# GpSimd makes five of the low parts of w_out's second half between and behind its last low parts of w_in

## The reference, cut to what matters

```python
proj = x @ w_in                                  # 1024 -> q | k | v | g | bg | cg | hc, 512 each
q, k = rotary(q), rotary(k) * HEAD_DIM ** -0.5
o, s_ret_new = retention(q, k, v, s_ret)         # chunks for the new stream, one block for the running ones
ret_out = groupnorm(o) * silu(g) * beta_ret
u = cg * hc
z = conv_b + sum(conv_w[t] * upad[:, t:t + L] for t in range(3))
conv_out = bg * z * beta_conv
m = concat([ret_out, conv_out]) @ w_out          # 1024 x 1024
h = layer_norm1(alpha * x + m)
y = layer_norm2(alpha * h + moe(h))              # moe: top 4 of 32, two matrices of 1024x2048 and 1024x1024 each
```

## Time and profile before

| | us |
|---|---|
| median of 3 runs | 1122.45 (1121.52 to 1122.66) |
| the profiled execution: its time | 1123.92 |
| the profiled execution: its span | 1122.1 |

### The profile page before, as it was taken

The page is one execution under the profiler, slowest core; times in us unless marked ns, Lnnn a source line. Parts: engine busy times, 40 slices in busy tenths (PEclk is TensorE's granted clock), DMA queues, the critical chain, the costliest instruction groups (busy, mean ns, idle before and its releaser), DMA issues.

```text
span 1122.1 us, 13598 instructions
## 1 busy us (share of the span) xinstructions
PE 1077.4 (96%) x5552; PEld 543.1 (48%) x5552; DVE 332.1 (30%) x596; ACT 199.1 (18%) x344; POOL 103.0 (9%) x58
## 2 busy tenths in 40 slices
PE   9999999999999999999999999999998989898994
PEld 6889968344434343434443434343434343433431
DVE  3487984512131212121213021212131313121114
ACT  3244213120112020202010102020111111111101
POOL 4675550000000000000000000000000000000002
PEclk9999999999999999999999999999999999999998
DMA  9970298999999999999999999999999999999993
GB/s 351 323 236 1 87 383 339 427 425 427 426 428 428 427 426 429 427 427 428 430 427 429 429 427 428 429 429 428 429 429 426 428 430 429 428 429 428 425 428 143
DMA packets 55748, 436.28 MB, mean 389 GB/s; under 512 B 8032, under 2 KB 18016, under 8 KB 28992
## 3 DMA queue, kind: packets, MB, share of 16 engines
q1 hardware_dynamic: 49184, 428.68, 91.8%
q10 hardware_dynamic: 6528, 7.09, 1.8%
HBM read 431.78 MB, written 3.97 MB: 388 GB/s over the span
## 4 chain that ended last, share of the span: by engine, by line
PE 63%; DMA 27%; DVE 1%; ACT 0%; POOL 0%; issue 0%; DVEq 0%; SPq 0%; ACTq 0%; POOLq 0%
DMA ring<-w_down 24%; PE bank L989 24%; PE bank L1015 17%; PE bank L925 8%; PE bank L622 4%; DMA old_rooms<-w_down 3%; PE bank L1038 1%; PE bank L833 1%; PE bank L1040 1%; PE bank L970 1%; PE bank L998 1%; PE bank L758 1%; PE bank L823 1%; DVE mixed_lo L1521 0%; PE bank L796 0%; PE bank L772 0%
## 5 line engine op out<-in xcount | busy, mean ns | idle before, releaser
L989 PE MATMUL bank<-ring,xg 128*64 128x512 f32 x1536 | 345.5, 595 | 8.9 <-DMA ring<-w_gu 8.9
L989 PEld LDWEIGHTS bank<-ring,xg 128*64 128x64 f32 x1536 | 105.2, 136 | 211.8 <-issue 186.5
L1015 PE MATMUL bank<-ring,act_t 128*64 128x512 f32 x672 | 150.8, 595 | 8.0 <-DMA ring<-w_down 8.0
L989 PE MATMUL bank<-old_rooms,xg 128*64 128x512 f32 x496 | 112.4, 595 | 5.0 <-DMA old_rooms<-w_gu 5.0
L1720 DVE SCALAR_TENSOR_TENSOR oo_lo<-oo_raw,gate_s,oo_hi 128x512 fp32r<-128x512 f32 x32 | 24.0, 751 | 312.7 <-ACT oo_hi L1247 312.7
L1748 DVE TENSOR_SCALAR gate_c<-bank 128x512 f32<-128x512 f32 x32 | 22.1, 692 | 258.6 <-PE bank L989 258.6
L925 PEld LDWEIGHTS bank<-onehot,hid 128*128 128x128 f32 x720 | 85.9, 196 | 12.2 <-issue 12.2
L1015 PEld LDWEIGHTS bank<-ring,act_t 128*64 128x64 f32 x672 | 46.2, 137 | 92.0 <-issue 78.0
L1324 POOL TENSOR_TENSOR rstd<-veps,minus_half 128x1 f32<-128x1 f32 x6 | 3.3, 546 | 949.3 <-DVE veps L1512 949.3
L925 PE MATMUL bank<-onehot,hid 128*128 128x128 f32 x720 | 88.8, 283 | 0.0
L1734 DVE TENSOR_TENSOR xy<-xy,bank 128x512 f32<-128x512 f32 x84 | 52.7, 683 | 107.6 <-PE bank L1040 107.6
(11 more groups left out here) (237 smaller groups left out, 951.1 us busy)
## 6 DMA issues: line engine op xcount, KB each, us to landing
ring<-w_gu SPq DMA_DIRECT2D x90, 2048.0 KB, 30.6
ring<-w_down SPq DMA_DIRECT2D x41, 2048.0 KB, 33.0
old_rooms<-w_gu SPq DMA_DIRECT2D x30, 2048.0 KB, 31.9
old_rooms<-w_down SPq DMA_DIRECT2D x13, 2048.0 KB, 33.0
ring<-w_in SPq DMA_DIRECT2D x13, 1024.0 KB, 14.2
ring<-w_gu SPq DMA_DIRECT2D x12, 1024.0 KB, 10.0
old_rooms<-w_down SPq DMA_DIRECT2D x6, 1024.0 KB, 16.6
over_q<-w_down SPq DMA_DIRECT2D x3, 2048.0 KB, 19.2
```

Of the source, the lines that this page charges most:

```text
L989: mm = pe.matmul(bank[2 * a + n][64 * hf:64 * hf + 64, :], xg[:, c, 64 * a:64 * a + 64], w[:, col:col + 512], start=False, stop=(c == KC - 1))
L1015: mm = pe.matmul(bank[b][64 * hf:64 * hf + 64, :], act_t[:, a, c % 4, 64 * (c // 4):64 * (c // 4) + 64], w[:, c % run, hf * 512:(hf + 1) * ...
```

## The change

The low parts of w_out's second half lose their place behind the wait for `conv_ready`. Each now waits for its own high part. GpSimd makes chunk 0 before half 25 of w_in, chunk 1 behind it, chunk 2 between halves 26 and 27, chunks 3 and 4 behind half 27 and ahead of `v_streams`, and chunks 5, 6 and 7 behind `v_streams`. The instructions are the same ones, in the same number.

```diff
-            low_parts(*range(8, 26))
+            def out_low_parts(*chunks):
+
+                for c in chunks:
+                    pool.wait_ge(out_hi_ready, KC + c + 1)
+                    r, o = out_words(1, c)
+                    pool.tensor_tensor(out_lo(1, c), room(r)[:, o], out_hi(1, c).bitcast(F32), ALU.subtract)\
+                        .then_inc(out_lo_ready[1], 1)
+
+            low_parts(*range(8, 25))
+            out_low_parts(0)
+            low_parts(25)
+            out_low_parts(1)
             for t in range(NT):
                 pool.wait_ge(gn_var, t + 1)
                 pool.tensor_tensor(grs[:, t, :], gve[:, t, :], minus_half[:, 0:H], ALU.pow).then_inc(gn_rstd, 1)
-            low_parts(26, 27)
+            low_parts(26)
+            out_low_parts(2)
+            low_parts(27)
+            out_low_parts(3, 4)
...
-            pool.wait_ge(conv_ready, CT)
-            pool.wait_ge(out_hi_ready, 2 * KC)
-            for c in range(KC):
-                r, o = out_words(1, c)
-                pool.tensor_tensor(out_lo(1, c), room(r)[:, o], out_hi(1, c).bitcast(F32), ALU.subtract)\
-                    .then_inc(out_lo_ready[1], 1)
+            out_low_parts(5, 6, 7)
```

## The result

| | before | after |
|---|---|---|
| median of the runs, us | 1122.55 (6 runs) | 1126.53 (6 runs) |
| ratio to before | | 1.0036, 95% interval 1.0026 to 1.0047 |
| the profiled execution: time, span | 1123.92, 1122.1 | 1127.16, 1125.4 |

The change makes the kernel 4.0 us slower. The forecast was 1125.0 with a range up to 1126.3: the way was right, the size was 1.5 us short, and the time lies outside the range.

A forecast was written before the change was run, and what follows sets the result against it. Bound: the DMA weight flow at 427 GB/s, whose restart waits for TensorE's last mixer matmul. `streams(0)` +3.9 us, with the old idle gone `streams(2)` +2.6: 1122.45 + 2.6 = 1125.0 us, range 1121.6 to 1126.3.

The forecast's parts named there:

- the place and the price of the taps: VectorE's convolution: each low part meeting a tap with two SBUF inputs costs up to 1.1 us, as for `mixed_lo`.
- Eight taps: VectorE's taps L1486, beside chunks 5 to 7 and the router's two products: held up by 4.1 us in all.
- the four first taps: VectorE's L1482, start of the convolution, beside chunks 3 and 4 and the masked copies: last one ends 1.7 us later.
- the keys: VectorE's three `kk`, which TensorE wants at 120.56: they end in time, so 0 lost, at worst +1.4 us.
- The idle at `streams(2)`: TensorE's 1.24 us idle ahead of `streams(2)` goes once the low parts leave the second four `mixed_lo`: -1.3 us.
- the step from `streams(0)` to `streams(2)`: TensorE in the mixer: from 151.4 at its old speed without the old idle, `streams(2)` at 158.7, +2.6 us.
- the stored states: Loads issued at 182.13 wait for them; they move later with TensorE, so the 0.7 us of cover is not subtracted.
- chunks 0 and 1: GpSimd before and behind half 25: the three `kk` go first, end near 117.5, nothing lost: 0.
- rival C: Tap delays plus GpSimd first at 115.8, `kk` +1.4 us: end moves by up to 4.0, 1126.5 us; chance 0.10.
- A: Taps L1486 not held up beside GpSimd, `conv_ready` at 147.3: 1121.5 us, faster but within 0.2%; chance 0.14.
- D: VectorE keeps its turn for all eight taps, `conv_ready` near 148.3, nothing changes at the end: about 1122.2; chance 0.08.
- B: The forecast itself: taps take turns with GpSimd, `conv_ready` near 151, 1125.0 us, spanning 1123.6 to 1126.0; chance 0.68.

## Why the prediction was wrong

*Right: the place and the price of the taps.* That a low part of w_out holds a tap up as it holds `mixed_lo` up was taken from the place of the inputs, since no row showed it. It measured 1.53 to 1.66 us beside a chunk and 0.87 to 0.98 beside a router's product, against 0.63 alone. Eight taps cost 3.6 us more (4.1 forecast), the four first taps 2.0 more (1.7 forecast, since a first tap takes 1.46 us beside a chunk and not 1.2), and 0.2 us had been lost before, at the keys (0 forecast). `streams(0)` was put at 151.4 and came at 151.46; that it fits to 0.1 us is partly luck, since these three errors, -0.5, +0.3 and +0.2, cancel. The idle at `streams(2)` went.

*Wrong: the step from `streams(0)` to `streams(2)`, "151.4 + (154.8 - 147.54) = 158.7".* The forecast gave TensorE an idle of nearly 4 us and then let it work on at the speed of before. `streams(2)` came 5.3 us later than before and not 2.6, because behind that idle the granted clock was at half for some 6 us of full work, worth 2.7 us between `streams(0)` and `streams(1)`. The sentence behind it, that all that follows up to 186.29 moves by the same amount, held: the four issues moved by 5.3 us too. Filling the idle gives the forecast's move back, 1124.2 against 1121.7; putting the same idle in by another wait gives most of the loss without the change (+3.6 us). The kernel before held the hint: its own idle at this place was 1.24 us, the clock 1.00 through the mixer, and the row "granted clock" was never asked what would become of an idle three times as long. The Trainium skill has the rule (TensorE: Matmul & The Clock Gate, What's actually happening): the throttled clock is the default state and activity releases it. The runs agree at `streams(0)`, 3.5 us idle and then 0.51. That rule belonged among the rivals and was not there. The half clock near 232 us, with TensorE busy in the record, stays unexplained.

*Wrong in part: the stored states.* The forecast let their landing move with TensorE and took nothing off. They landed some 10 us earlier than before instead, and the end moved by 4.0 us (3.3 in the profiled executions) where TensorE's last mixer matmul moved by 5.3. Without that early landing the miss would have been larger. With the idle filled, where TensorE moved by 2.6, the end moved by 2.5, as the forecast has it.

*Wrong, at no price: chunks 0 and 1.* The three `kk` did not all go first: GpSimd's chunk 0 took its turn behind the first one (1.50 us, not 2.9), they ended at 120.80 and not near 117.5, and TensorE waited 0.15 us and was 0.2 us late from there on. That is rival C with a seventh of its price of 1.4 us. The four `mixed_lo` of the run with chunks 5 to 7 late kept GpSimd waiting for all four again (first chunk 2.95 us). Why one run of VectorE's instructions lets GpSimd in and the other doesn't stays open.

*Rivals.* A (no hold-up) falls by the taps' durations and D (VectorE keeps its turn) by their alternation. Up to `streams(0)` the runs bear B out. The measured 1126.53 is the figure given for C, 1126.5, just above the range's end of 1126.3, but that is luck: C's delay at the keys was 0.2 us, and the rest came from the clock, which no rival had.

## What to carry to other kernels

GpSimd's elementwise work, which reads SBUF, cost VectorE nothing in this case only where VectorE had an input in PSUM (0.69 us for `hid<-bank,lnp`, 1.22 for `st<-st,bank`); beside instructions with all their inputs in SBUF it cost VectorE 0.9 to 1.1 us for each low part of 128x512. Before moving such work into a gap of GpSimd's queue, look at what VectorE does in that gap and who waits for it. And a new wait of TensorE has two prices: its length, and, at the 3.5 us and more measured here, the slow stretch behind it, so a stall that is forecast has to be followed by the question at which clock the work behind it runs. A delay and a lead of the same size need not weigh the same where another resource restarts behind them.

## What the runs showed of the hardware

- An idle of TensorE of 3.50 to 3.57 us was followed, in all three records of it, by some 6 us of full work at half clock (granted clock 0.51 and 0.52), one of 6.62 us by some 6.5 us of it (0.51). Idles of 1.24 and 1.62 us left it at 1.00. At 2.93 us one record has it at 1.00 and the spread of the times suggests that it mostly was not. The clock also fell once without an idle, near 232 us, in five of the thirteen records.
- Matmuls whose result nobody reads, in the idle, kept the clock at 1.00 and gained 1.5 to 2.0 us.
- A VectorE instruction with two SBUF tensor inputs, of the two kinds seen here (TENSOR_TENSOR, SCALAR_TENSOR_TENSOR), takes turns with GpSimd instructions that read SBUF, at about 1.0 us for each GpSimd subtraction of 128x512; a memset beside it costs nothing (0.62 us against 0.63). A TENSOR_SCALAR with its one tensor input in SBUF waits for memsets as well (2.12 us; alone it takes 478 ns for 400 elements).
